# Five projection chunks of the second block by seven block products each in place of eight, with the rotation of the dilated heads left on GpSimd

## What is computed

```python
def token_mixer(xn, w_in, b_forget, q_norm_fox, k_norm_fox, q_norm_dil, k_norm_dil, ...):
    proj = xn @ w_in                                   # 256x1024 @ 1024x(6*512 + 8)
    qa, ka, va = jnp.split(proj[..., :o1], 3, axis=-1)     # "fox" heads, 8 of 64
    qb, kb, vb = jnp.split(proj[..., o1:o2], 3, axis=-1)   # "dilated" heads, 8 of 64
    fa = proj[..., o2:]                                    # 8 forget logits
    qa = rmsnorm(heads(qa, N_HEADS_FOX), q_norm_fox)
    ka = rmsnorm(heads(ka, N_HEADS_FOX), k_norm_fox)
    logf = jax.nn.log_sigmoid(fa + b_forget)
    oa = forgetting_attention(qa, ka, va, logf)
    qb = rope(rmsnorm(heads(qb, N_HEADS_DIL), q_norm_dil), pos)
    kb = rope(rmsnorm(heads(kb, N_HEADS_DIL), k_norm_dil), pos)
    ob = dilated_attention(qb, kb, vb)
    return jnp.concatenate([rmsnorm(oa), rmsnorm(ob)], axis=-1) @ w_out
```

## Time and profile before

| | us |
|---|---|
| median of 3 runs | 940.83 |
| lowest and highest | 938.72, 941.16 |
| the profiled execution, whole | 941.74 |
| its span in the trace | 939.9 |

### The profile page before, as it was taken

The page is one execution under the profiler, slowest core; times in us unless marked ns, Lnnn a source line. Parts: engine busy times, 40 slices in busy tenths (PEclk is TensorE's granted clock), DMA queues, the critical chain, the costliest instruction groups (busy, mean ns, idle before and its releaser), DMA issues.

```text
span 939.9 us, 21235 instructions
## 1 busy us (share of the span) xinstructions
PE 797.7 (85%) x9499; PEld 553.4 (59%) x9499; DVE 230.8 (25%) x618; ACT 182.9 (19%) x389; POOL 66.5 (7%) x76
## 2 busy tenths in 40 slices
PE   7999999999999999999999787867675576765665
PEld 4555588885676654446757665746454464544543
DVE  2132830231522231533535111101001010010101
ACT  2012322330412132205725020102010020100100
POOL 6200300000000130250000000000000000000000
PEclk9999999999999999999999999989899797898977
DMA  9984624049899999532657999999999999999995
GB/s 306 329 320 180 230 107 180 1 166 420 327 395 416 403 366 335 204 155 90 253 217 288 429 426 425 425 427 425 430 429 427 430 427 428 430 427 431 427 428 243
DMA packets 55557, 310.16 MB, mean 330 GB/s; under 512 B 5426, under 2 KB 7178, under 8 KB 43088
## 3 DMA queue, kind: packets, MB, share of 16 engines
q1 hardware_dynamic: 50848, 301.60, 79.9%
q0 software_dynamic: 2912, 4.37, 1.5%
q10 hardware_dynamic: 1744, 3.41, 0.9%
HBM read 307.76 MB, written 4.19 MB: 332 GB/s over the span
## 4 chain that ended last, share of the span: by engine, by line
PE 64%; DMA 32%; issue 2%; DVE 1%; ACT 0%; DVEq 0%; SPq 0%
PE ps L1718 60%; DMA ring<-in_w_up 22%; DMA ring<-in_w_down 5%; DMA ring<-in_w_gate 5%; PE ps L1744 1%; PE ps L2046 1%; PE ps L1899 1%; DMA xx<-in_x 0%; PE ps L1758 0%; PE ps L2089 0%; PE ps L1775 0%; PE ps L1861 0%; PE ps L1766 0%; PE ps L1939 0%; ACT arena L854 0%
## 5 line engine op out<-in xcount | busy, mean ns | idle before, releaser
L1718 PE MATMUL ps<-ring,arena 128*32 128x128 f32 (+1 forms) x4832 | 207.4, 313 | 93.8 <-DMA ring<-in_w_gate 42.9
L1718 PEld LDWEIGHTS ps<-ring,arena 128*32 128x32 f32 (+1 forms) x4832 | 160.5, 123 | 139.2 <-DMA ring<-in_w_gate 51.3
L1718 PE MATMUL ps<-ring,xx 128*128 128x512 f32 (+2 forms) x384 | 157.5, 567 | 0.0
L1718 PE MATMUL ps<-arena 32*128 32x256 f32 (+9 forms) x1332 | 126.1, 365 | 3.3 <-issue 1.7
L1718 PEld LDWEIGHTS ps<-ring,xx 128*128 128x128 f32 x384 | 72.5, 192 | 76.1 <-issue 72.3
L1718 PEld LDWEIGHTS ps<-arena 32*128 32x128 f32 (+4 forms) x1332 | 81.7, 167 | 35.1 <-issue 29.8
L1718 PE MATMUL ps<-ring,const 128*32 128x256 f32 x864 | 57.7, 408 | 25.6 <-DMA ring<-in_w_down 23.1
L1718 PE MATMUL ps<-xx,ring 128*128 128x256 f32 x288 | 64.9, 382 | 0.0
L1718 PEld LDWEIGHTS ps<-xx,ring 128*128 128x128 f32 x288 | 53.8, 190 | 8.0 <-issue 0.7
L1718 PEld LDWEIGHTS ps<-ring,const 128*32 128x32 f32 x864 | 28.0, 115 | 51.6 <-issue 32.8
L1718 PE MATMUL ps<-ring,xs 128*128 128x512 f32 x96 | 43.3, 607 | 0.0
(11 more groups left out here) (317 smaller groups left out, 662.1 us busy)
## 6 DMA issues: line engine op xcount, KB each, us to landing
ring<-in_w_up SPq DMA_DIRECT2D x37, 2048.0 KB, 25.1
ring<-in_w_gate SPq DMA_DIRECT2D x36, 2048.0 KB, 23.6
ring<-in_w_down SPq DMA_DIRECT2D x32, 2048.0 KB, 23.8
ring<-in_w_in SPq DMA_DIRECT2D x15, 2048.0 KB, 20.5
arena<-in_w_down SPq DMA_DIRECT2D x6, 2048.0 KB, 12.3
ring<-in_w_out SPq DMA_DIRECT2D x4, 2048.0 KB, 8.4
arena<-in_w_gate SPq DMA_DIRECT2D x4, 2048.0 KB, 15.7
arena<-in_w_up SPq DMA_DIRECT2D x2, 2048.0 KB, 17.4
```

What stands on the lines that cost most here:

```text
L1718: ins = pe.matmul(dst, w, x, start=start, stop=stop, skip_group_check=True)
```

## The change

Each of the first five chunks, a product C = A B with A of 256x1024 and B of 1024x512, is formed by the seven products of Strassen and Winograd over quarters: A in quarters of 128 tokens by 512 features, B in quarters of 512 features by 256 columns. A product is then four matmuls of 128x128 by 128x256, and a chunk is 28 of these in place of 16 of 128x512. Chunk six is as before.

- **DVE** forms four sums of quarters of x once (`x_sum`, 128x512 each) and four sums of quarters of the weights in each chunk (`weight_sum`, 128x1024 each), two of them in place in the ring slot. The first sum of a chunk is formed a chunk ahead, that of chunk one at the end of the first mixture of experts.
- **ACT** brings five results a chunk out of PSUM (`out_of_psum`, 128x256), three of them partial contents of a bank to which PE then goes on adding, so that PE waits for each (`s_sev`). DVE adds the two remaining banks and one partial result (`add_second`, `add_third`, `add_part`).
- **Moved:** the heads' squares go from DVE to ACT (`head_squares`); the forget rows of `aug_r2` go from DVE to ACT; the log sigmoid's first two steps now stand on ACT between the first and the second result of chunk one. The first half of chunk six's first tile goes ahead of the fox transposes. The load into place -5 waits until all five chunks are done, since its columns hold sums now, and comes third in its row.
- **Unchanged:** `rope` on POOL, and everything behind it. In the first block three semaphores are merged into one.

```diff
-            for n in (2, 0, 1, 3, 4):
+            load_moe2(0, 0, FIRST2[0], q1)
+            load_moe2(1, 0, FIRST2[1], q1)
+            sp.wait_ge(s_prod, 7 * 5)
+            for n in (2, 3, 4):
                 load_moe2(n, 0, FIRST2[n], q1)
...
+            def out_of_psum(dst, c, product, b, tt):
+                act.wait_ge(s_prod, 7 * c + product)
+                return act.activation(dst, bank(b, T), ACT.Copy, scale=x_rstd[:, tt:tt + 1])
...
+                out_of_psum(dst[:, 0, 0:T], c, 1, bx, 0).then_inc(s_sev, 1)
+                if ahead:
+                    ahead()
+                out_of_psum(dst[:, 0, T:2 * T], c, 3, bx, 0).then_inc(s_sev, 1)
+                out_of_psum(c22_part[c % 2], c, 4, bz, 1).then_inc(s_sev, 1)
+                out_of_psum(dst[:, 1, T:2 * T], c, 5, bx, 1).then_inc(s_sev, 1)
+                if behind:
+                    behind()
+                out_of_psum(dst[:, 1, 0:T], c, 7, bx, 1).then_inc(s_pev_a, 1)
...
+            chunk(0, q2_tm, ahead=forget_abs_exp)
...
+            def weight_sum(c, j, q):
...
+                out, x, y = {1: (t1, b12, b11), 2: (t2, b22, t1), 3: (b12, b22, b12), 4: (b21, b21, t2)}[j]
+                dve.tensor_tensor(out, x, y, ALU.subtract).then_inc(s_tsum, 1)
...
+            add_second(v_tm, 4)
+            weight_sum(4, 4, q1)
+            dve.wait_ge(s_pev_a, CH_BG + 4)
+            dve.wait_ge(s_pev_d, 6 + 4)
+            dve.wait_ge(s_dn, 1)
+            head_sums(10)
+            add_part(v_tm, 4)
+            add_third(v_tm, 4)
+            head_factors("fox", arena[:, 0:2048]).then_inc(s_hn, 1)
...
+                product(bx, xnT[:, 0:4, 0:P], w[:, 0:4, left], True, False)
+                if between:
+                    between()
+                product(by, xnT[:, 4:8, 0:P], w[:, 4:8, left], True, True)
+                pe.wait_ge(s_sev, 4 * c + 1)
+                pe.wait_ge(s_asum, 2)
+                pe.wait_ge(s_tsum, 4 * c + 2)
+                product(bx, a_sum[1], t2, False, False)
+                product(bz, a_sum[0], t1, True, False)
+                pe.wait_ge(s_sev, 4 * c + 2)
+                pe.wait_ge(s_asum, 3)
+                pe.wait_ge(s_tsum, 4 * c + 3)
+                product(bx, a_sum[2], w[:, 0:4, right], False, False)
+                pe.wait_ge(s_sev, 4 * c + 3)
+                pe.wait_ge(s_asum, 4)
+                product(bz, a_sum[3], w[:, 4:8, right], False, True)
+                pe.wait_ge(s_sev, 4 * c + 4)
+                pe.wait_ge(s_tsum, 4 * c + 4)
+                product(bx, xnT[:, 4:8, P:T], w[:, 4:8, left], False, True)
...
+            first_v2_tile(0, 4)
+            pe.wait_ge(s_hn, 2)
+            pe.wait_ge(s_aug, 4)
+            head_transposes(q_tm, k_tm)
+            first_v2_tile(4, KD).then_inc(s_proj, 1)
```

More of the change, by code:

```diff
@@ L1034, in _ @@
             act.wait_ge(s_rs, FACTORS["x2"])
[L1035 to L1060, removed]
@@ new lines, in forget_abs_exp, with forget_rows @@
+            def forget_abs_exp():
+                act.wait_ge(s_fl, F_BIASED)
+                act.activation(f_l, f_z, ACT.Abs).then_inc(s_fl, 1)
+                act.wait_ge(s_fl, F_ABS)
+                act.activation(f_l, f_l, ACT.Exp, scale=-1.0).then_inc(s_fl, 1)
+            def forget_rows(dst2, parts, scale):
+                for p0, e in parts:
+                    act.activation(dst2[p0:p0 + AH, e],
+                                   bank(4, T)[p0:p0 + AH].unsqueeze(1).broadcast_to([AH, AH // 2, T]),
+                                   ACT.Copy, scale=scale).then_inc(s_aug, 1)
@@ new lines, in _ @@
+            chunk(0, q2_tm, ahead=forget_abs_exp)
+            act.wait_ge(s_fl, F_EXP)
+            act.activation(f_l, f_l, ACT.Ln, bias=1.0).then_inc(s_fl, 1)
+            chunk(1, k2_tm, ahead=lambda: head_squares(arena[:, 20 * 256:24 * 256], 0, 1))
+            chunk(2, q_tm, ahead=lambda: head_squares(arena[:, 24 * 256:28 * 256], 1, 2),
+                  behind=lambda: root(ROOTS["dil"]))
+            act.wait_ge(s_fl, F_SUMS)
+            act.wait_ge(s_clr, 64)
+            forget_rows(aug_l2, ((96, 0), (32, 1)), 1.0)
@@ new lines, in _ @@
+            chunk(3, k_tm, ahead=lambda: head_squares(arena[:, 0:4 * 256], 0, 3))
+            forget_rows(aug_r2, ((64, 0), (0, 1)), -1.0)
+            chunk(4, v_tm, ahead=lambda: head_squares(arena[:, 4 * 256:8 * 256], 1, 4),
+                  behind=lambda: root(ROOTS["fox"]))
+            act.wait_ge(s_htp, 3)
+            for e in range(2):
+                half = slice(DH * e, DH * e + DH)
+                act.activation(aug_l2[half, e], tiles4(4)[half], ACT.Copy,
+                               scale=gcol[half, R_FQ:R_FQ + 1]).then_inc(s_hT_a, 1)
@@ L1640, in _ @@
                                          op1=ALU.add).then_inc(s_fl, 1)
[L1642 to L1669, removed]
@@ new lines, in _ @@
+            weight_sum(0, 4, q1)
+            for j in (1, 2, 3):
+                weight_sum(1, j, q1)
+            add_part(q2_tm, 0)
+            add_third(q2_tm, 0)
+            add_second(k2_tm, 1)
+            dve.wait_ge(s_fl, F_LN)
+            dve.scalar_tensor_tensor(out=f_log, in0=f_z, scalar=0.0, in1=f_l, op0=ALU.min,
+                                     op1=ALU.subtract).then_inc(s_fl, 1)
+            weight_sum(1, 4, q1)
+            for j in (1, 2, 3):
+                weight_sum(2, j, q1)
@@ new lines, in _ @@
+            for j in (1, 2, 3):
+                weight_sum(4, j, q1)
+            add_part(k_tm, 3)
+            add_third(k_tm, 3)
+            add_second(v_tm, 4)
[7 more added lines that the diff above has]
+            head_factors("fox", arena[:, 0:2048]).then_inc(s_hn, 1)
+            dve.wait_ge(s_htp, 4)
@@ L1670, in _ @@
+            for e in range(2):
+                half = slice(DH * e, DH * e + DH)
+                dve.tensor_scalar(aug_r2[half, e], tiles4(6)[half], gcol[half, R_FK:R_FK + 1], None,
+                                  ALU.mult).then_inc(s_hT_d, 1)
             dve.wait_ge(s_htp, 6)
@@ new lines, in _ @@
+            chunk(0, forget_logits)
+            chunk(1)
+            pe.wait_ge(s_fl, F_LOG)
+            upto = const[:, C_UPTO:C_UPTO + P]
+            for o0 in (0, 32, 64, 96):
+                dst = bank(4, T)[o0:o0 + AH]
+                mm(dst[:, 0:P], f_log[:, 0:AH], upto, True, True)
+                mm(dst[:, P:T], f_log[:, 0:AH], ones, True, False)
+                ins = mm(dst[:, P:T], f_log[:, AH:2 * AH], upto, False, True)
+            ins.then_inc(s_fl, 1)
+            for c in range(2, 5):
+                chunk(c)
```

182 lines of the change are left out of this document (136 added, 46 removed).

## The result

The changed kernel's median is 934.11 us (933.12 to 934.93, 4 runs) against 940.77 for the kernel before in the same comparison: ratio 0.9931, interval 0.9917 to 0.9945, or 5.2 to 7.8 us less. I had forecast 3.2 us less and a time of 937.6, range 934.3 to 941.8.

A forecast was written before the change was run, and what follows sets the result against it. PE's own work was taken as the bound up to 507 us: 7.5 gained in products, less 1.7, 0.6 and 2.0 of stalls, makes 3.2 us less than the median 940.83, so 937.6 us, range 934.3 to 941.8.

The forecast's parts named there:

- PE as the bound, and one for one: Up to 507 us PE's own work sets the end, so PE's gain in the changed stage arrives one for one.
- The products: Five chunks on PE: 12.3 us each instead of 13.8, 61.5 instead of 69.04 together, a gain of 7.5 us.
- The rival that more is lost in PE: Waits inside chunks cost 0.1 us each, or the clock falls after a stall: 938.8 to 940.8 us, chance 0.2.
- Sums and transfers in the chunks: DVE's sums and additions and ACT's transfers in the five chunks stay hidden beside 12.3 us of PE a chunk.
- the case of late weights: Chunk one's weights landing at the slowest, 348.0 us, would hold x back by 3 us; taken as hidden.
- Chunk one's stall: Before product five PE waits for ACT's transfer behind the absolute value and exponential: 1.7 us lost.
- The wait ahead of chunk six: Chunk six uses chunk five's bank and waits for its last transfer: 0.6 us lost.
- The fox heads' factors: Behind chunk five, POOL's rotation holds DVE's three tiny steps and scaling for 3.9 us; PE stalls 2.0 (ends 0 and 3).
- Fewer stalls: Rival: tiny steps aren't held (2.0 us gained) or ACT's chain is shorter (up to 1.7): 933.9 to 935.9 us, chance 0.2.
- The rotation: POOL's rotation, slowed by DVE's two-input work, ends at 424.9 us, PE wants it at 428.3: hidden, 3 us to spare.
- The slower rival: DVE and POOL exclude each other in every instruction, so PE is 6.9 us later: 944.5 us, chance 0.08.
- The load into place -5: It moves from early in its stage to the end, where DMA is half idle; read after 507 us: costs nothing.

The follow-up runs named there:

- second comparison: The changed kernel run again unaltered against the kernel before: median 936.06 us, ratio 0.9955 (0.9934 to 0.9977).
- c1: Changed kernel plus eight tiny dependent DVE steps behind chunk four's last addition, beside POOL's rotation; forget logits' parts to dilated transposes 81.87 us, changed kernel 75.94.
- a3: Changed kernel with the forget logits' absolute value and exponential on ACT moved behind chunk one's fourth transfer; ratio to the kernel before 0.9910, median 933.33 us.
- a4: Changed kernel with POOL's rotation replaced by one small copy; forget logits' parts to dilated transposes 75.95 us, whole time (median 1405.69) not comparable.
- b1: As a3, and chunk six's first tile no longer waits for ACT's last transfer of chunk five; ratio to the kernel before 0.9911, median 932.65 us.

## Why the prediction was right or wrong

**PE as the bound, and one for one:** right in kind. The stage gained 5.4 us and the first comparison 5.2 to 7.8, the second 2.2 to 6.2. About 1 us of the stage's gain seems to be given back in the tail.

**The products:** right. I took 12.3 us a chunk and 12.2 were measured; the five groups of waits in a chunk cost nothing that can be seen. That is 0.6 us of the miss.

**The rival that more is lost in PE** (0.1 us for every group of waits, or a lower clock after a stall) didn't come: the waits cost nothing, and the granted clock was 1.00 through the whole stage. Its second half is real all the same: I had a fall at 1.4 us, and in c1, after a stall of 2.67 us, it cost 3.1. What a stall of 2.0 us would have done here no run shows.

**Sums and transfers in the chunks:** hidden, as said, also at ACT's tight places. The first sum of chunk one started at 343.05 without waiting for its weights, so the case of late weights didn't occur. These instructions each took a little longer than I had it: 1.22 us for a sum of weights (1.15), 0.69 for one of x (0.6), 0.47 for a transfer (0.36) and 0.42 to 0.48 for an addition (0.35).

**Chunk one's stall:** the mechanism was right and a3 shows it; 1.35 us instead of 1.7. DVE's logits were out 7.1 us after chunk one began, by my count, and the absolute value started at 357.05, 7.2 after. Product five started 9.3 us after chunk one began, against 9.4 by my sum. The stall was shorter because PE was ready for product five 0.3 us later than I had it: it had done product four at 357.85, which is 8.0 us after chunk one's start, against 7.7.

**The wait ahead of chunk six:** 0.61 against 0.6.

**The fox heads' factors, the step that failed:** I let the chain begin at 63.8 us after chunk one's start (measured 63.45) and gave it 3.9 us of being held by POOL, so that PE would stall for 2.0. It was held for 1.9 us: 0.14, 0.95, 0 and 0.79 for its three tiny steps and the scaling, where I had 0.6, 1.1, 1.1 and 1.1. The exclusion is real (a4), and a tiny step is mostly held as well (c1, six in eight); the error was to take it for certain every time, in a chain of only four, and to have the first at half an instruction. With a chain 2 us shorter the scaling ended 0.2 us before PE came, and the whole term fell away. That it fell away entirely is luck of 0.2 us, as b1 shows. It is 2.0 of the 2.2 us by which the stage was better than forecast. I had named 0 and 3 as the ends of this term, and *Fewer stalls* with 933.9 to 935.9 as its rival, with a chance of 0.2. That is the case that came by its size; its condition, that tiny steps aren't held, came only in part, since the chain was held for half of what I had. The range's lower end cut this rival at 934.3 where it should have taken it in whole. The stage alone would put the first comparison at 940.77 - 5.44 = 935.33, inside the range; the other 1.2 us of its median don't lie in the stage, and the second comparison doesn't repeat them.

The sum in terms of the stage: forecast 3.2; products +0.6, chunk one's stall +0.35, the rest of chunk one -0.7, fox term +2.0, gives 5.45, against 5.44 measured. Chunk one took 14.6 us to the end of its seventh product; 12.2 for the products and 1.35 of idle leave 1.05, of which the logits between the products had cost 0.37 before too.

**The rotation:** hidden, with 4.2 us to spare against 3. That DVE would be held in its weight sums, about turn about, was right: four sums and POOL's instructions alternate from 394.43 to 403.30.

**The slower rival** (every instruction of DVE excluded) didn't occur: the additions with one operand in PSUM took 0.47 to 0.48 beside POOL and without it. The Trainium skill (SBUF — State Buffer, section Who interferes with whom) has it that a VectorE instruction with at most one input in SBUF, outside the modes that use both its ports, doesn't contend with GpSimd; these additions have one in SBUF and one in PSUM, and the traces agree.

**The load into place -5** I called free. By the tails it isn't quite: about 1 us, without a mechanism.

## What to carry to other kernels

Where two engines exclude each other instruction by instruction, a chain of tiny dependent steps can pay up to one instruction of the other engine a step (1.03 us a step in c1, 1.1 us for three steps in the fox chain), but whether that costs anything depends on the slack at its end; work out the slack with the chain's price at both ends, and let the range take in both results. Price the stall too: in c1 an idle of 2.67 us cost PE 5.8, because the granted clock fell behind it.

When seven products replace eight and PE is the limit, the gain is close to the eighth's own time (a chunk went from 13.8 to 12.2 us here, and an added product cost 1.73), less what new hand-overs add: look for the transfer that stands behind something slow (a table load) in an in-order queue, and move that. After a stall is taken away, the next chain may lie only tenths behind it, as b1 showed.

## What the runs showed of the hardware

- VectorE steps of 128x32 with two operands in SBUF, each waiting for the one before, run 0.23 us apart alone and 1.03 us apart beside GpSimd tensor_tensor instructions of 1.1 to 1.3 us (and one of 2.4); six of eight were held, five of them for a whole instruction or nearly one.
- VectorE's sums of 1024 elements with two operands in SBUF took 1.22 us alone and 2.01 to 2.63 beside the rotation, while a scalar_tensor_tensor with one operand in PSUM took 0.47 to 0.48 in both cases.
- After 2.67 us without a matmul PE's granted clock fell from 1.00 to its lower level, 0.50 (1.2 GHz), from 416 to 422 us, and eight records of 128x512 took 5.55 us instead of 3.51 (c1); after idles of 1.35 and 0.61 us it stayed at 1.00.
- PE's granted clock was 0.79 over 8 us (76 to 84) in one execution of the kernel before, among matmuls without idle, and 1.00 in that stretch of all the other traces.
